# Attention of a hybrid diffusion layer: query-state products as three rounded part products, two gate slots, and a new order on VectorE and ScalarE

## What is computed

```
q, k, v, o, ig, fg, u, ga, gb = split(h @ w_in)
h_f, state_f = mlstm(q, k, v, gates_f, context then latent)
h_b, state_b = mlstm(reversed ...)
    D   = b_t - b_s + log_i_s          (masked)
    wts = exp(D - m_t);  sc = exp(m_prev + b - m_t)
    num = (q k^T * wts) v + sc * (q C)   # C: the state before this chunk
    den = row sums of the same, with the state vector n
    C   = a C + g (k * ew)^T v
    h   = num / max(|den|, exp(-m_t))
hm = rmsnorm(h_f + h_b) * g_head * sigmoid(o)
x  = x + gt1 * rmsnorm((sigmoid(ga) * (hm @ w_br_a) + sigmoid(gb) * (pool(u) @ w_br_b)) @ w_out)
x  = x + gt2 * rmsnorm(ConvFFN(x))
```

## Time and profile before

| what | value |
|---|---|
| runs of the kernel | 1732.57, 1731.26, 1730.47 us; median 1731.26 us |
| profiled execution | 1731.23 us, of it span 1729.4 us from first to last instruction |
| granted TensorE clock | 1.000 of full speed |
| PE busy | 1717.7 us (99%) |
| PEld, DVE, ACT, POOL busy | 1621.4 (94%), 1266.2 (73%), 703.2 (41%), 256.4 us (15%) |
| chain that ended last | PE 91%, DVE 4%, DMA 2%, ACT 1% |

### The profile page before, as it was taken

The page is one execution under the profiler, slowest core; times in us unless marked ns, Lnnn a source line. Parts: engine busy times, 40 slices in busy tenths (PEclk is TensorE's granted clock), DMA queues, the critical chain, the costliest instruction groups (busy, mean ns, idle before and its releaser), DMA issues.

```text
span 1729.4 us, 27434 instructions
## 1 busy us (share of the span) xinstructions
PE 1717.7 (99%) x10568; PEld 1621.4 (94%) x10568; DVE 1266.2 (73%) x2754; ACT 703.2 (41%) x1300; POOL 256.4 (15%) x255
## 2 busy tenths in 40 slices
PE   9999999999999999999999999999999999999998
PEld 3999999999999999999988899999999999888787
DVE  4776777687678766563455589888888888788898
ACT  4543222343234253451343554433344443444354
POOL 1010000000100100010000062444433333100000
PEclk9999999999999999999999999999999999999999
DMA  9214433344334445374242331333322221787876
GB/s 347 73 49 137 94 116 113 117 128 124 110 113 160 124 142 166 136 247 128 74 146 85 110 103 66 111 107 107 98 77 76 76 68 63 224 263 228 263 252 241
DMA packets 216279, 236.21 MB, mean 137 GB/s; under 512 B 11568, under 2 KB 160828, under 8 KB 216148
## 3 DMA queue, kind: packets, MB, share of 16 engines
q1 hardware_dynamic: 200916, 179.54, 34.1%
q0 software_dynamic: 10752, 38.00, 6.5%
q10 hardware_dynamic: 4480, 16.91, 2.4%
HBM read 181.49 MB, written 52.92 MB: 136 GB/s over the span
## 4 chain that ended last, share of the span: by engine, by line
PE 91%; DVE 4%; DMA 2%; ACT 1%; SPq 1%; issue 1%; POOL 0%; ACTq 0%; DVEq 0%; POOLq 0%
PE ps L1476 23%; PE ps L1105 13%; PE ps L1106 12%; PE ps L1107 12%; PE ps L1418 6%; PE ps L1493 4%; PE ps L1494 4%; PE ps L1495 4%; PE ps L1283 2%; PE ps L1299 2%; PE ps L1300 1%; PE ps L1301 1%; PE ps L1134 1%; DMA w_sub<-z_w_diff 1%; PE ps L1128 1%; DMA adaw<-in_w_ada_dram 1%
## 5 line engine op out<-in xcount | busy, mean ns | idle before, releaser
L1105 PE MATMUL ps<-H_hi,ring_hi 128*128 128x384 f32 x1200 | 405.5, 338 | 0.4 <-DVE H_lo L2214 0.2
L1107 PE MATMUL ps<-H_hi,ring_lo 128*128 128x384 f32 x1200 | 401.1, 334 | 0.0
L1106 PE MATMUL ps<-H_lo,ring_hi 128*128 128x384 f32 x1200 | 401.1, 334 | 0.0
L1105 PEld LDWEIGHTS ps<-H_hi,ring_hi 128*128 128x128 f32 x1200 | 225.4, 188 | 1.9 <-DVE H_lo L2214 1.7
L1106 PEld LDWEIGHTS ps<-H_lo,ring_hi 128*128 128x128 f32 x1200 | 225.5, 188 | 0.2
L1107 PEld LDWEIGHTS ps<-H_hi,ring_lo 128*128 128x128 f32 x1200 | 225.3, 188 | 0.0
L1476 PE MATMUL ps<-T_hi,up_hi 128*128 128x288 f32 x608 | 130.5, 296 | 0.5 <-ACT held_g L2049 0.4
L2214 DVE TENSOR_TENSOR up_lo<-up_raw,up_hi 128x512 fp32r<-128x512 f32 x114 | 88.4, 778 | 57.2 <-ACT up_hi L2007 57.2
L1476 PE MATMUL ps<-T_lo,up_hi 128*128 128x288 f32 x608 | 130.2, 296 | 0.0
L1476 PE MATMUL ps<-T_hi,up_lo 128*128 128x288 f32 x608 | 130.1, 296 | 0.0
L1493 PE MATMUL ps<-B_hi,A_hi 128*128 128x512 f32 x308 | 120.3, 391 | 0.8 <-DVE A_lo L2214 0.7
(11 more groups left out here) (349 smaller groups left out, 3763.3 us busy)
## 6 DMA issues: line engine op xcount, KB each, us to landing
raw<-in_w_in_dram SPq DMA_DIRECT2D x44, 512.0 KB, 4.2
up_raw<-in_w_up_dram SPq DMA_DIRECT2D x38, 512.0 KB, 5.2
w_raw<-in_w_down_dram SPq DMA_DIRECT2D x66, 256.0 KB, 3.3
raw<-in_w_ada_dram SPq DMA_DIRECT2D x32, 512.0 KB, 5.1
X<-z_f SPq DMA_DIRECT2D x44, 256.0 KB, 3.8
GE<-z_gates SPq DMA_DIRECT2D x72, 128.0 KB, 3.8
w_sub<-in_w_down_dram SPq DMA_DIRECT2D x33, 256.0 KB, 3.9
z_w_diff<-w_raw SPq DMA_DIRECT2D x22, 256.0 KB, 2.8
```

Of the source, the lines that this page charges most:

```text
L1105: pe.matmul(out, whi, xhi, start=first, stop=False)
L1106: pe.matmul(out, whi, xlo, start=False, stop=False)
L1107: return pe.matmul(out, wlo, xhi, start=False, stop=last)
```

## The change

It has four parts.

1. From step 2 on the product of the weighted queries with the state is three fp32r products of 258 columns in place of one fp32 product of 257. VectorE makes the parts: `Cst_hi`, `qs_hi` (rounding copies), `Cst_lo`, `qs_lo` (differences). Step 1 keeps the fp32 product.
2. The gates have two slots in place of three, and are loaded behind the next unit's weights; the room goes to the new tiles. `Cst_hi` lies over the context state `Cctx`, so VectorE waits in step 2 until that has been stored. `qs_hi` lies over a part of `SC` that is then no longer copied (step 1 copies two of four parts).
3. VectorE forms the weights of a step first, then the next gates, the turned head, `lo_split`, and the modulation products last. Ahead of the attention, in unit 8, the pooling work and `lo_split` come before the modulation products. TensorE sums a modulation column behind the first block of the unit, not ahead of it.
4. ScalarE rounds the values before `hi_split`, and `exps` (exponential and, where due, square roots) comes behind the third block, no longer behind the first.

The slots of tiles after the attention are also counted from another start (`slot`), which goes with the memory layout.

```
-    GSLOTS = 3
+    GSLOTS = 2
...
-                if it[0] == "unit" and 0 <= it[1] - SEG < NT * NH:
-                    gates_load(it[1] - SEG)
+                if it[0] == "unit" and 0 < it[1] - SEG <= NT * NH:
+                    gates_load(it[1] - SEG - 1)
...
-                if i:
-                    mm = pe.matmul(ps[:, 5 + d, 0:VW], qs[:, d, :], Cst[:, d, :], start=False, stop=True)
+                if i == 1:
+                    mm = pe.matmul(ps[:, 5 + d, 0:VW], qs[:, d, :], Cst[:, d, 0:VW], start=False, stop=True)
+                elif i:
+                    pe.matmul(ps[:, 5 + d, 0:VP], qs_hi[:, d, :], Cst_hi[:, d, :], start=False, stop=False)
+                    pe.matmul(ps[:, 5 + d, 0:VP], qs_hi[:, d, :], Cst_lo[:, d, :], start=False, stop=False)
+                    mm = pe.matmul(ps[:, 5 + d, 0:VP], qs_lo[:, d, :], Cst_hi[:, d, :], start=False, stop=True)
...
-                if m in ADA_AT:
-                    ada_sum(ADA_AT[m])
+                if m == RU:
+                    ada_sum(ADA0)
...
+                    if b == 0 and m > RU and m in ADA_AT:
+                        ada_sum(ADA_AT[m])
...
-                    evac_main(act, q0, qT[idx % 2], QSCALE, exps)
+                    evac_main(act, q0, qT[idx % 2], QSCALE, exps, NB - 1)
...
-                    evac_main(act, q0, stage[st], 1.0, exps)
+                    evac_main(act, q0, stage[st], 1.0, exps, NB - 1)
...
+                if i > 1:
+                    link(ins)
+                    if i == 2:
+                        dve.wait_ge(new_state_stored, 64 * (h + 1))
+                    dve.wait_ge(att_state, 2 * e)
+                    dve.tensor_copy(Cst_hi[:, :, :], Cst[:, :, :])
+                    link(dve.tensor_copy(qs_hi[:, :, :], qs[:, :, :]))
+                    sub_hi(Cst_lo[:, :, :], Cst[:, :, :], Cst_hi[:, :, :])
+                    ins = sub_hi(qs_lo[:, :, :], qs[:, :, :], qs_hi[:, :, :])
```

More of the change, by code:

```diff
@@ L173, in build, with slot @@
     load_of = {it: w for w, it in enumerate(loads)}
+    def slot(w):
+        return (w + LS - 1) % LS
     sigmoids = [it for it in loads if it[0] != "hm"]
@@ L263, in build @@
     Pt_hi = place("Pt_hi", [P, 2, P], F32R)
+    v_lo = place("v_lo", [P, 2, DV], F32R)
     v_hi = place("v_hi", [P, 2, VP], F32R, at=VT0)
-    v_lo = place("v_lo", [P, 2, DV], F32R, at=VT0 + (8 * VP + 31) // 32 * 32)
+    Cst_lo = place("Cst_lo", [P, 2, VP], F32R, at=VT0 + (8 * VP + 31) // 32 * 32)
     a_tok = place("a_tok", [P, NT, 2, NH])
@@ L268, in build @@
     ST0 = base[0]
-    Cst = place("Cst", [P, 2, VW])
+    Cst = place("Cst", [P, 2, VP])
     Cctx = place("Cctx", [P, 2, VW])
+    Cst_hi = place("Cst_hi", [P, 2, VP], F32R, at=base[0] - 2080)
     AT0 = base[0]
@@ L275, in build @@
     qs = place("qs", [P, 2, P])
+    qs_lo = place("qs_lo", [P, 2, P], F32R, at=base[0] - 1024)
     SC = place("SC", [P, SEEN, 4, P])
+    qs_hi = place("qs_hi", [P, 2, P], F32R, at=base[0] - 2048 * SEEN + 1024)
     ada_part = place("ada_part", [P, 2, P])
@@ L1020, in _ @@
                         pool.wait_ge(tile_used, KD + e + 1)
-                pool.dma_start(tiles[:, w % LS, :], Z[what][d]).then_inc(tile_in[w % LS], 16)
+                pool.dma_start(tiles[:, slot(w), :], Z[what][d]).then_inc(tile_in[w % LS], 16)
             pool.wait_ge(mix_sum, NB)
@@ L1890, in _ @@
                     act.wait_ge(att_weights, seg + 1)
-                    act.activation(SC[:, seg % NT - 1, :, :], ps[:, 3, :].rearrange("p (a b) -> p a b", b=P),
+                    parts = 2 if seg % NT == 1 else 4
+                    act.activation(SC[:, seg % NT - 1, 0:parts, :], ps[:, 3, 0:parts * P].rearrange("p (a b) -> p a b", b=P),
                                    ACT.Copy).then_inc(att_cached, 1)
@@ L2222, in lo_split @@
                 if s == S_OUT + WO - 1:
-                    dve.wait_ge(tile_used, KD + 1 + max(d for d in range(KD) if load_of[("ga", d)] % LS == LS - 1))
+                    dve.wait_ge(tile_used, KD + 1 + max(d for d in range(KD) if slot(load_of[("ga", d)]) == LS - 1))
                 hi, lo = split_of(s)
@@ L2452, in ada_products, with head_turned @@
                             ins.then_inc(ada_mac, 1)
+            def head_turned(h, j):
+                item = ("hm", 2 * h + j)
+                st = stage[stage_no[item] % 2]
+                dve.wait_ge(o_sigmoid, item[1] + 1)
+                dve.wait_ge(evac0, 3 * use_of[item] + 3)
+                dve.scalar_tensor_tensor(out=st[:, :], in0=st[:, :], scalar=vT[:, V_GH + item[1]:V_GH + item[1] + 1],
+                                         in1=work[j][:, :], op0=ALU.mult, op1=ALU.mult).then_inc(head_staged, 1)
             def gate_branch_b(d):
@@ L2503, in _ @@
                     continue
-                if m + 1 in ADA_AT:
-                    ada_products(ADA_AT[m + 1])
                 if mains[m - 1][0] == "u":
                     pool_group(mains[m - 1][1])
-                if m > RU and not (kind == "v" and idx % 2):
+                if RU < m < SEG:
                     lo_split(m + 2)
+                if m == SEG - 1:
+                    ada_products(ADA_AT[SEG])
                 if m == SEG - 1:
@@ L2530, in _ @@
                     attention_weights(h, i)
+                    if seg + 1 < NT * NH:
+                        gate_arguments(seg + 1)
+                    if m in TURN_AT:
+                        head_turned(*TURN_AT[m])
+                    if not (kind == "v" and idx % 2):
+                        lo_split(m + 2)
+                    if m + 1 in ADA_AT:
+                        ada_products(ADA_AT[m + 1])
                     if m - 1 in NORM_AT:
```

37 lines of the change are left out of this document (15 added, 22 removed).

## The result

The changed kernel takes **1737.53 us** in the median of six runs (1736.27 to 1738.55), the kernel before 1731.64 beside it (1730.05 to 1732.68): a ratio of 1.0036, 95% interval 1.0026 to 1.0046. It is 5.9 us slower; 4.4 were forecast (1735.7 us). In a later series, five runs of it had a median of 1737.79 us against 1731.40, a ratio of 1.0041 (1.0027 to 1.0054). The profiled execution took 1737.78 us, its span is 1736.0.

What follows compares the result with a forecast made beforehand. TensorE, busy 99% of the span, was taken as the bound. The terms -3.9 + 0.6 + 1.9 + 2.5 + 3.1 + 0.2 gave +4.4 us, so 1735.7 us; 8 in 10 range 1728 to 1742.

Steps and rivals of the forecast that it cites:

- Term A: Product of queries and state on TensorE, steps 2 to 8: three part products save 0.07 us each, 3.9 us in all.
- VectorE's added work: Copies and differences for the parts, 1.8 us per step, claimed hidden in VectorE's 3.23 us wait for TensorE's values.
- The price set on its absence: If VectorE's cover were gone, each lacking tenth would cost 2.8 us over 28 steps.
- Term B: Unit 8, ahead of the attention: pooling group first waits for the pooling product, so everything ends later, +0.6 us.
- Term C: Heads 1 and 2: TensorE's scores wait for ScalarE's late copy to `SC`, +1.9 us (step 2) and +2.5 (step 3).
- Term D: Head 3, step 3: turning head 2 waits for the scaling, held by late square roots, +3.1 us.
- The extra 0.2 for step 3: Head 3, step 3: remaining wait for the copy of the scores after the turn, +0.2 us (0 to 0.6).
- The table load: ScalarE's table load in terms C and D, taken at its row's 1.28 us, not the skill page's 2.66 per switch.
- Rival 1: ScalarE's copies and roots behind the third block come in time, so no slowdown: 1728.0 or 1726.5 us; chance 0.17.
- Rival 2: VectorE becomes the bound; 0.3 us lacking in each of 28 steps adds 8.4 us, 1744.1 us; chance 0.14.
- Rival 3: A ScalarE table switch costs about twice its row, +6.4 us on top, 1742.1 us; chance 0.04.

Runs made afterwards that it cites:

- the second execution: The changed kernel, unaltered, profiled once more in a later series beside the kernel before: median 1737.79 us, ratio 1.0041.
- the first experiment: The changed kernel with exponential and square roots behind a unit's second block, no longer the third: 1728.98 us, ratio 0.9985 to the kernel before.

## Why the prediction was right, and what it lacked

**Term A held.** 3.9 us forecast, 3.5 measured (3.4 by the steps). Three part products stand 0.12 us apart as worked out; the changed kernel, step 3 of head 1:

```profile
363.37 0.28 PE L1288 MATMUL ps<-v_hi,Pt_lo 128*128 128x258 f32 x1
363.49 0.28 PE L1292 MATMUL ps<-Cst_hi,qs_hi 128*128 128x258 f32 x1
363.60 0.28 PE L1293 MATMUL ps<-Cst_lo,qs_hi 128*128 128x258 f32 x1
363.72 0.29 PE L1294 MATMUL ps<-Cst_hi,qs_lo 128*128 128x258 f32 x1
363.84 0.29 PE L1296 MATMUL ps<-v_hi,kw_hi 128*128 128x258 f32 x1
```

**VectorE's added work was hidden**, as said. The price set on its absence was not: 2.2 us more per step cost 2.8 us in all, not 2.8 for each tenth.

**Term B held.** 0.6 forecast; the second execution is 0.04 us late at the first unit and 0.67 at the first values, so 0.63.

**Term C: step 2 held, step 3 was too dear.** Against the first experiment the two steps lose 1.08 and 0.94 us, in two heads 4.0; forecast were 0.95 and 1.2, together 4.4. In step 3 I let the store wait for the exponential; it does not, and the price came out near the lower bound, 0.8. The list's 0.81 is a little less than the price, since it counts from the end of a row; from T to their start the scores of step 3 take 3.15 us, against 2.17 in the first experiment, so they come 0.98 later.

**Term D held without its echo.** The wait of 2.97 us costs 3.2 in its step; 3.1 + 0.2 were forecast. The extra 0.2 for step 3 did not come: that copy, whose store does not wait for the exponential either, ends at 653.81 us, and the turn holds the scores back until 654.06.

**What failed** is the step from wait to price. A wait was counted at its length, and the list of terms ended there. In four profiles of five with a wait of 2.9 to 4.0 us at the turn the granted clock fell to 1.2 GHz behind it; in the changed kernel the scores and the unit's first matmuls then ran at about half speed, which cost 1.6 us. Added up: 1.1 for order (0.65 of it B), 3.5 gained, 4.0 for C, 3.2 for D make 4.8 us; with the fall of the clock in every execution it is 6.4. Measured are 5.9 and 6.4. That this comes so close is in part luck, as the forecast's 4.4 was: A was 0.4 too high and C 0.4 too dear, which cancels, and the differences of single executions near 34 us and in the ConvFFN, up to 2 us each, stand in neither sum. The Trainium skill ("TensorE: Matmul & The Clock Gate", "HAM oscillation — how this bites in real kernels") describes this: a wait ahead of matmuls after which the next group starts at the lower clock. These traces agree in that, with 0.50 granted behind waits of 2.97 and 3.98 us. The waits of its example are longer than the 2.97 us here, and there the measurement decides: 2.9 to 3.0 us were enough in three executions and not in a fourth. This section of the Trainium skill, not the one on table loads, was the one to weigh.

**The table load** was rightly taken from its row. At 347.74 it starts 0.43 us behind the start of an exponential of 0.41, lasts 1.28, and the roots start at its end, 349.03. The 2.66 us of the Trainium skill ("ScalarE: Activation LUTs", "What ACT_TABLE_LOAD costs") are not seen at any of the five places.

**The rivals.** Rival 1 is false as forecast: the load stood behind the third block. Rival 2 is false in the changed order, but it stands close by: with the old order and the late roots TensorE waited for `v_lo`. Rival 3 is false.

## What to carry to other kernels

Where TensorE never waits, ask of each moved instruction what stands behind it in its own queue and when that is due. The square roots were cheap anywhere but between a bank's last use and the copy that frees it, and one block earlier they cost nothing. And count a wait of some two microseconds or more on TensorE as more than its length, since the clock may fall behind it, as it did here.

## What was not expected of the hardware

- After a wait of 2.97 us the granted clock fell to 0.50 in one execution of a kernel and stayed at 1.00 in another of the same. The price was 1.6 us. After 3.98 us of waiting it was some 2.5: the step lost 6.59, and by the other's 3.06 for 2.97 it would have been 4.07.
- Near 33 to 38 us, behind a pause of TensorE of only 0.35 to 0.40 us, the clock fell in five of the thirteen profiled executions, among them one of the two of the changed kernel; behind a like pause of 0.35 to 0.39 us it stayed at 1.00 in five others. It costs 1.7 us, more than a quarter of the difference that was to be explained. All five are the changed kernel or versions of it; neither of the two profiles on the code of the kernel before has the fall. Whether the change makes it more frequent is open.
- In step 3 of head 1 a store that ScalarE issues goes out beside a table load, 0.01 us behind its start, and ahead of the exponential that waits for the table.
